# The last pair of an attention's parts: exponentials stand, values move, and the result is transposed behind the last z tile

## What is computed

```
z  = h @ w_in
s  = concat([q k_local + bias, q k_context])          # per head, 256 + 256 keys
p  = softmax(s)
ya = (p_local @ v_local + p_context @ v_context) * silu(z[A_Z])
yb = short_conv_branch(z)
yc = conformer_branch(z)                              # with a layer norm
ga, gb, gc = sigmoid(z[GATES])
m  = ga * (ya @ w_out_a) + gb * (yb @ w_out_b) + gc * (yc @ w_out_c)
x  = x + gate * (m @ w_o)
```

## Time and profile before

| | |
|---|---|
| median of 3 runs | 841.13 us (840.89 to 841.98) |
| profiled execution | 840.87 us, of which the span from first to last instruction is 839.0 us |
| TensorE | busy 834.2 us (99%), 7168 matmuls |
| VectorE | busy 656.0 us (78%) |
| ScalarE | busy 509.9 us (61%) |
| GpSimd | busy 51.2 us (6%) |
| granted TensorE clock | full in all 40 slices of the span |
| mean of DMA | 196 GB/s |

### The profile page before, as it was taken

How to read it: one execution, slowest core, us unless ns; L and a number is a source line. 1 busy time by engine, 2 the same in 40 slices (tenths; PEclk the granted TensorE clock), 3 DMA queues, 4 the chain that set the end, 5 groups by cost and what they waited for, 6 DMA issues and landing times.

```text
span 839.0 us, 17524 instructions
## 1 busy us (share of the span) xinstructions
PE 834.2 (99%) x7168; PEld 812.0 (97%) x7168; DVE 656.0 (78%) x1236; ACT 509.9 (61%) x928; POOL 51.2 (6%) x72
## 2 busy tenths in 40 slices
PE   9999999999999999999999999999999999999998
PEld 8999999999999897899999999999999999999998
DVE  6989778898977789786678555566799889997873
ACT  4796887764435568678778444434547685444650
POOL 0003000000000126100000000021020000000000
PEclk9999999999999999999999999999999999999999
DMA  9945877888986824378757856617555424456541
GB/s 306 320 151 192 271 247 255 265 270 278 302 271 220 283 73 130 102 222 244 211 178 217 239 185 200 195 59 179 169 181 163 140 78 150 152 173 194 166 150 51
DMA packets 161826, 164.23 MB, mean 196 GB/s; under 512 B 16801, under 2 KB 158289, under 8 KB 161489
## 3 DMA queue, kind: packets, MB, share of 16 engines
q1 hardware_dynamic: 160656, 162.05, 61.3%
q10 hardware_dynamic: 1088, 1.05, 0.4%
HBM read 162.01 MB, written 2.91 MB: 197 GB/s over the span
## 4 chain that ended last, share of the span: by engine, by line
PE 96%; DVE 2%; issue 0%; ACT 0%; POOL 0%; DVEq 0%; POOLq 0%
PE ps L316 25%; PE ps L318 25%; PE ps L320 25%; PE ps L1653 2%; PE ps L1649 2%; PE ps L1651 2%; PE ps L484 2%; PE ps L1742 1%; PE ps L1746 1%; PE ps L1744 1%; PE ps L1700 1%; PE ps L1711 1%; PE ps L453 1%; PE ps L1691 1%; DVE wl L283 1%; PE ps L467 1%
## 5 line engine op out<-in xcount | busy, mean ns | idle before, releaser
L283 DVE TENSOR_TENSOR wl<-raw,wh 128x1024 fp32r<-128x1024 f32 x259 | 315.2, 1233 | 23.0 <-ACT wh L276 22.9
L316 PE MATMUL ps<-xh,wh 128*128 128x256 f32 x1160 | 325.4, 280 | 0.1
L320 PE MATMUL ps<-xh,wl 128*128 128x256 f32 x1160 | 321.8, 277 | 0.8 <-DVE wl L283 0.7
L318 PE MATMUL ps<-xl,wh 128*128 128x256 f32 x1160 | 321.6, 277 | 0.2
L276 ACT ACTIVATE wh<-raw 128x1024 fp32r<-128x1024 f32 x259 | 269.8, 1051 | 74.3 <-PE ps L320 67.8
L316 PEld LDWEIGHTS ps<-xh,wh 128*128 128x128 f32 x1160 | 217.9, 188 | 4.4 <-issue 2.8
L320 PEld LDWEIGHTS ps<-xh,wl 128*128 128x128 f32 x1160 | 218.3, 188 | 1.5 <-DVE wl L283 1.4
L318 PEld LDWEIGHTS ps<-xl,wh 128*128 128x128 f32 x1160 | 217.9, 188 | 0.7 <-DVE xl L399 0.5
L320 PE MATMUL ps<-hh,wl 128*128 128x256 f32 x512 | 141.3, 276 | 0.0
L316 PE MATMUL ps<-hh,wh 128*128 128x256 f32 x512 | 141.3, 276 | 0.0
L318 PE MATMUL ps<-hl,wh 128*128 128x256 f32 x512 | 141.3, 276 | 0.0
(11 more groups left out here) (357 smaller groups left out, 1357.6 us busy)
## 6 DMA issues: line engine op xcount, KB each, us to landing
raw<-in_w_in_dram SPq DMA_DIRECT2D x34, 1024.0 KB, 5.4
raw<-in_mlp_up_dram SPq DMA_DIRECT2D x32, 1024.0 KB, 5.7
raw<-in_mlp_down_dram SPq DMA_DIRECT2D x32, 1024.0 KB, 7.1
aw<-in_w_adaT_dram SPq DMA_DIRECT2D x24, 512.0 KB, 4.9
raw<-in_rec_w_in_dram SPq DMA_DIRECT2D x7, 1024.0 KB, 10.7
raw<-in_att_w_in_dram SPq DMA_DIRECT2D x6, 1024.0 KB, 6.0
raw<-in_rec_w_out_dram SPq DMA_DIRECT2D x4, 1024.0 KB, 5.6
raw<-in_att_w_o_dram SPq DMA_DIRECT2D x4, 1024.0 KB, 5.5
```

The costliest lines, as they stand in the source:

```text
L283: e.tensor_tensor(parts_of(i)[1], raw_of(i), f32(parts_of(i)[0]), op=ALU.subtract).then_inc(S["wl"], 1)
L316: e.matmul(o, H[:, first + n], xh[:, k], start=start and n == 0, stop=False)
L318: e.matmul(o, H[:, first + n], xl[:, k], start=False, stop=False)
L320: ins = e.matmul(o, L[:, first + n], xh[:, k], start=False, stop=stop and n == len(ks) - 1)
```

## The change

For pair n = 7 alone the operands change places. `tensor_weighted_last` has the exponentials standing (`PT2[i]`, 128 keys x 128 queries) and the values moving (64 columns), four key blocks for each of the two parts, and writes queries on the partitions and 2 x 64 features along the free axis (`valrows`). ScalarE copies that to `SL[1]` in the place where it made the high part of `ya7`. `tensor_weighted_turn`, at the formerly empty step k = 19 behind z tile 23, transposes it in one matmul into the second quarter of the same PSUM bank. VectorE's product of pair 7, ScalarE's high part and VectorE's low part follow later: the product and the high part behind the loop over the z tiles, the low part in the first round of the first branch, behind that round's three weight low parts. The other seven pairs are as before.

```diff
--- before.py
+++ after.py
@@ -1713,11 +1713,34 @@
                 if j == 3:
                     ins.then_inc(closing(f"vals{2 * n + i}", p[:, 0:128]), 1)
 
+    def tensor_weighted_last(e, q):
+
+        p = main(q, (S["yam"], 8))
+        q.wait_ge(S["pt2"], 16)
+        q.wait_ge(S["vx"], 8)
+        for i in range(2):
+            h = part(14 + i)[0]
+            for j in range(4):
+                ins = e.matmul(p[:, 64 * i:64 * i + 64], PT2[i][:, j * 128:(j + 1) * 128],
+                               (VL, VX)[j // 2][:, j % 2, 64 * h:64 * h + 64], start=j == 0, stop=j == 3)
+        ins.then_inc(closing("valrows", p), 1)
+
+    def tensor_weighted_turn(e, q):
+
+        p = ps["valrows"]
+        q.wait_ge(S["pt2"], 17)
+        e.matmul(p[:, 128:256], SL[1][:, 0:128], ident, is_transpose=True).then_inc(closing("vals15", p[:, 128:256]), 1)
+        ps["vals14"] = p[:, 128:256]
+
     def tensor_attend(e, q, k):
+        if k == 19:
+            tensor_weighted_turn(e, q)
         if k % 2:
             return
-        if 4 <= k < 20:
+        if 4 <= k < 18:
             tensor_weighted2(e, q, (k - 4) // 2)
+        if k == 18:
+            tensor_weighted_last(e, q)
         if 2 <= k < 18:
             tensor_flip2(e, q, k - 2)
             tensor_flip2(e, q, k - 1)
@@ -1992,7 +2015,7 @@
 
     def vector_late(e, q, k):
 
-        if 5 <= k < 21 and k % 2:
+        if 5 <= k < 19 and k % 2:
             vector_ya_low(e, q, (k - 5) // 2)
         if 0 < k <= len(ZS) - 4 and ZS[k + 3][0] == "bz":
             vector_yb_low(e, q, ZS[k + 3][1])
@@ -2003,6 +2026,8 @@
             for f in (2 * j, 2 * j + 1):
                 lows(e, q, ahead(f"m{i}.{f}")[1])
             lows(e, q, ahead(f"out{i}.{j}")[1])
+            if b == 0 and j == 0:
+                vector_ya_low(e, q, 7)
             for f in (2 * j, 2 * j + 1):
                 gate = T2.of[f"gt{b}.{f}"][0]
                 q.wait_ge(S["gt"], 8 * b + f + 1)
@@ -2128,6 +2153,7 @@
                 vector_attend(e, q, i - 4)
             vector_convolve(e, q, 1 if 1 <= i < 4 else 2 if 4 <= i and i % 2 else 3)
         vector_late(e, q, len(ZS) - 4)
+        vector_outputs2(e, q, 7)
         for b in range(3):
             vector_branch(e, q, b)
         assert conv["n"] == len(TAPS)
@@ -2172,6 +2198,11 @@
         free(q, freed)
         e.activation(t[:], src, ACT.Tanh, scale=0.5).then_inc(S["gt" if key[0] == "g" else "tg"], 1)
 
+    def scalar_ya_high(e, q, n):
+        rows = slice(128 * (n % 2), 128 * (n % 2) + 128)
+        q.wait_ge(S["yam"], n + 1)
+        e.activation(YAH[:, n // 2, rows], T2.of[f"ya{n}"][0][:, 0:128], ACT.Copy, scale=0.5).then_inc(S["yah"], 1)
+
     def scalar_attend(e, q, k):
         if k % 2 == 0:
             for i in (k - 2, k - 1) if 2 <= k < 18 else ():
@@ -2179,12 +2210,11 @@
                 if i > 1:
                     q.wait_ge(S["mm"], done[f"vals{i - 2}"])
                 e.activation(PT2[i % 2][:], ps[f"flips{i}"], ACT.Copy).then_inc(S["pt2"], 1)
-            if 4 <= k < 20:
-                n = (k - 4) // 2
-                rows = slice(128 * (n % 2), 128 * (n % 2) + 128)
-                q.wait_ge(S["yam"], n + 1)
-                e.activation(YAH[:, n // 2, rows], T2.of[f"ya{n}"][0][:, 0:128], ACT.Copy, scale=0.5).then_inc(
-                    S["yah"], 1)
+            if 4 <= k < 18:
+                scalar_ya_high(e, q, (k - 4) // 2)
+            if k == 18:
+                q.wait_ge(S["mm"], done["valrows"])
+                e.activation(SL[1][:, 0:128], ps["valrows"][:, 0:128], ACT.Copy).then_inc(S["pt2"], 1)
             for i in (k, k + 1) if k < 16 else ():
                 s = SL[i % 3]
                 q.wait_ge(S["lg2"], i + 1)
@@ -2300,6 +2330,7 @@
                 scalar_attend(e, q, i - 4)
             if name == "bz":
                 scalar_yb_high(e, q, t)
+        scalar_ya_high(e, q, 7)
         for b in range(3):
             scalar_branch(e, q, b)
         for f in range(8):
```

## The result

The changed kernel took 848.12 us (median of 4 executions, 848.04 to 848.39) beside 841.16 us of the kernel before on the same chip: 1.0084 of it, with a 95% interval of 1.0072 to 1.0096. It is slower by 7.0 us. The forecast was 840.2 and the range went to 842.4, so the result lies outside it, and beyond the dearest rival (843.0).

The account below looks back on a forecast made before the run. TensorE, 96% of the chain that ended last, was taken as the bound, through its stream of starts. Group 0.57 + turn 0.11 - faster pace 1.6 = -0.9 us from 841.13 gave 840.2; range 839.2 to 842.4.

Parts of the forecast that it names:

- the dearest rival: The rival "slower, later flip", at 843.0 us the slowest case priced; chance 0.10.
- slower, later flip: Behind L1770 the pace settles slow: 620 matmuls to the end pay 4.6 ns each, 2.8 us, total 843.0; chance 0.10.
- 12 of 12 behind a full transpose: In all 12 places behind a full 128x128 transpose the stream was fast; so 360 matmuls behind the turn gain 1.6 us.
- pace kept: Behind the single transpose of the turn the pace stays slow, gain missing, change costs 0.7 us: 841.8; chance 0.17.
- The group: Last weighted group (valrows): sixteen records at 0.112 us, 1.80 against 1.23, a loss of 0.57 us.
- columns set the pace: In the valrows group moving columns set the pace: 0.85 us instead of 1.80, total 839.3; chance 0.06.
- The turn: One transposing matmul behind the last z tile costs 0.11 us, without a wait for ScalarE's copy of valrows.
- Cover gone: Without the last z tile (24 matmuls, 2.7 us) ahead of it, the turn would cost some 0.6 us more.
- ScalarE and VectorE: Copies, ya7's high part and pair 7's product come later; a conversion slips 1.6 us or more; cost nothing on the path.
- the lead: TensorE reads the late weight conversion six split tiles on, over 10 us away; without that lead, up to 1.9 us.
- The layer-norm rival: At L1770 a longer wait for VectorE and GpSimd takes up to all of TensorE's 0.9 us lead: 841.0; chance 0.10.
- The 0.2% of the chances: Differences under about 0.2% (1.7 us) can't be told from none; faster 0.10, same 0.78, slower 0.12.

Follow-up runs that it names:

- run 600: Not a label of a run: in "instructions that run 600 us later", "run" is a verb and 600 us a time.

## Why the prediction was wrong, and where it was right

**The sum began at the change.** "Here counts what it does to the stream of TensorE starts" was right; that this stream is untouched ahead of the first changed instruction was assumed in every case and written nowhere. That is the step that failed, a term put at nothing without a reason: 6.5 of the 7.0 us arise 600 us earlier, where 1484 matmuls took 174.86 us for 168.36. The rival "slower, later flip" had the mechanism and the price for each matmul (4.6 ns; 6.50 us / 1484 is 4.4), but searched only the 620 matmuls downstream. The view that held the danger was on the table: a stream with two paces at one clock, whose choice I had by a pattern only. Its price, had it turned anywhere, is the length of the longest fast stretch, 1484 x 4.4 ns. I had read stretches by what stands ahead of them in the program, as if that fixed it; L348 has the same instructions ahead of it in both kernels.

**What is shown and what is open.** Shown: it belongs to the program, and every execution of one program agrees (five runs of the changed kernel with at most one operation added, all slow). It is not the changed attention as such: neither needed (two kernels with the old attention are slow) nor enough (four with the changed weighted group are fast). One transpose more at the entry turns it, in either direction. One operation at the end of the program and one warming matmul do not. Open: by what way instructions that run 600 us later have a say at 102 us. A difference of the instructions' places in memory, and so of their fetching, is a guess that no run here isolates, and the three shifts that I made, in either kernel, did not turn the pace. Nor does the time of a fetch tell it: the first packet of the instruction queue q8 behind L348 comes 1.1 to 3.1 us behind it where the pace is fast and 0.8 to 1.9 where it is slow. I leave it open.

**"12 of 12 behind a full transpose".** The forecast carried this to a single one, for -1.6 us; it got 0. All twelve were groups of two or more. The rival "pace kept" named just this and priced it at +0.7 of the sum; the local sum is +0.66. The rule itself fell too: L348, a pair of full transposes, has the slow pace behind it in the changed kernel and in five others, and in a sixth behind three. And its reason, that what stood ahead of a stretch decides, does not hold. What the 1.6 us are worth was right (40.897 against 42.485).

**The group.** 16 x 0.112 = 1.80 forecast, 1.79 measured; the loss of 0.57 is 0.564. Two rows with the same standing columns, one with less and one with more moving, bounded the unseen form. The rival "columns set the pace" is refuted twice, by these 112 ns and by the 58 ns with half the standing columns. The prediction called the old group cheap because its two heads run side by side. They do start together: its records come in pairs 6 to 7 ns apart, a pair every 109 ns (worked out from the start times). But 109 ns for two records of 64 standing columns is hardly less than two unpaired ones cost, 2 x 58 (with 64 columns moving, not 128), so nearly all of the cheapness is in the 64 standing columns. The same run shows that the dear entry, which the change removed, goes with them too: it is there without any pairing. The Trainium skill, "TensorE: Matmul & The Clock Gate", section "LDWEIGHTS (loading the stationary operand)", agrees roughly: a load takes its columns over 1.2 ns by it, 107 for 128 and, as an estimate from that page, 53 for 64; the steady steps measured are 112 and 58. The Trainium skill gives a gap by moving columns alone too (same page, section "Back-to-back issue gap"), but for the isolated matmul, and says there that in a stream of loads and matmuls both set the spacing. The trace agrees: 64 columns moved at 112 ns a record and at 58.

**The turn.** 0.11 forecast, 0.116 measured, no wait. Cover gone: "some 0.6 more" forecast, 0.54 measured (0.66 with the turn itself).

**ScalarE and VectorE.** The first gate tile starts at 720.37 where I had 713.6, so the forecast's times are to be read 6.8 later. The high part of ya7 then was due at 723.1 and came at 723.20; the conversion behind it, due some 1.6 late, was 1.8 late (723.42 for 714.77 + 6.8), and the lead held; the first gate sum, due at 727.4, came at 727.78. Alone, the deferral is 0.00. The layer-norm rival did not come: L1780 to L1793 takes 9.639 for 9.640. In the four runs with the fast pace behind the group or the turn it did not either; TensorE kept its lead there, 9.640 to 9.643.

**The 0.2% of the chances.** With block 1 fast the change is worth +0.6 us (841.78 beside 841.05, less the 0.11 of the added transpose), within it. The chances were right for the change's own work and wrong for the program.

## What to carry to other kernels

Before forecasting a small edit in a kernel bound by TensorE, count matmuls in equal stretches over the whole span. If the plain stream has two paces at one granted clock, an edit may turn a stretch far from it: give that case a chance of its own, at the price of the longest stretch (a gain where that has the slow pace, a loss where it has the fast one). Afterwards compare stretch by stretch from the beginning of the span, not from the change on; and before a change is judged by its total, run it once more with a harmless record added ahead of the turned stretch (here 848.1 against 841.8), and count its matmuls again, for the same record can turn a fast stretch slow (here 841.1 against 847.7).

A form that isn't in the trace can be priced to a few per cent by two neighbours that differ from it in one size each. For fp32 weights that are used once, count the standing columns.

## What the runs showed of the hardware

- A stream of float32r matmuls of 256 columns has two steady paces at a granted clock of 1.00 (the 2.4 GHz level): 113.3 and 117.8 ns, either held over the 1484 matmuls behind L348. The pace there is set within a few matmuls of the entry; elsewhere it also fell without one (L320 to L1649, 113.5 to 117.8).
- Programs that differ only in instructions that run 600 us later can take different paces at the same entry (kernel before, fast; with four transposes behind its last weighted group, slow). How is open.
- One record of an fp32 matmul costs 112 ns with 128 standing columns, whether 2 or 64 columns move. The steady step between starts is 111 to 112, and 58 to 59 with 64 standing; in the old group, 64 standing and 128 moving in pairs, 109 a pair.
- A turned pace can outweigh a stall: the kernel that waits 0.37 us ahead of its turn has the shorter local sum (126.87 against 128.02). Whether the wait or the place of the turn brought the fast pace is not shown; no run parts them.
